# A sorted-token gather cut by blocks: two blocks before the first expert, four between the first four expert steps

## What is computed

```python
scores = sigmoid(h @ w_router)                      # 16 experts in 4 groups of 4
best = argmax over groups of the sum of the two best (scores + b_router) in the group
_, idx = top_k(masked to the best group, 2)
gsel = scores at idx, divided by their sum
combine = one_hot(idx) * gsel                       # a weight for each token and expert
gate, up = split(einsum('ld,edf->lef', xs, w_gu), 2)
hid = silu(gate) * up * combine
out = einsum('lef,efd->ld', hid, w_down)
```

## Time and profile before

| what | value |
|---|---|
| median of the 3 runs | 2985.69 us (2975.92 to 2989.59) |
| the profiled execution | 2981.99 us, of it a span of 2980.2 us |
| mean granted TensorE clock | 0.914 of full speed |
| PE busy | 2643.8 us, 89% |
| DMA | 524.43 MB, 50% of the 16 engines' time on the main queue |

### The profile page before, as it was taken

The page is one execution under the profiler, slowest core; times in us unless marked ns, Lnnn a source line. Parts: engine busy times, 40 slices in busy tenths (PEclk is TensorE's granted clock), DMA queues, the critical chain, the costliest instruction groups (busy, mean ns, idle before and its releaser), DMA issues.

```text
span 2980.2 us, 30519 instructions
## 1 busy us (share of the span) xinstructions
PE 2643.8 (89%) x11934; PEld 1940.3 (65%) x11934; DVE 1462.1 (49%) x2288; ACT 745.8 (25%) x1255; POOL 805.2 (27%) x445
## 2 busy tenths in 40 slices
PE   5688989997997889899998877788999899989997
PEld 3687864445986678744457876676444599974444
DVE  7446443334549876533335578974333416650012
ACT  1132120002453442300014244423010233230111
POOL 3355300002443254000013558850000156500000
PEclk7789889998899999799998887897999999979999
DMA  7534639891330215388953321032989243428881
GB/s 269 170 113 126 201 111 353 323 348 62 105 111 29 71 57 170 113 311 323 350 186 119 128 74 34 20 123 97 350 323 361 100 130 112 141 100 281 297 298 47
DMA packets 291854, 524.43 MB, mean 176 GB/s; under 512 B 9472, under 2 KB 141056, under 8 KB 291328
## 3 DMA queue, kind: packets, MB, share of 16 engines
q1 hardware_dynamic: 288256, 519.33, 50.0%
q10 hardware_dynamic: 3456, 3.15, 0.3%
HBM read 517.73 MB, written 4.72 MB: 175 GB/s over the span
## 4 chain that ended last, share of the span: by engine, by line
PE 75%; DVE 12%; issue 4%; DMA 3%; ACT 3%; POOL 2%; SPq 0%; DVEq 0%; ACTq 0%
PE ps L1755 23%; PE ps L1770 11%; PE ps L1547 6%; PE ps L1549 6%; PE ps L1548 6%; PE ps L1581 3%; DVE macc L1840 3%; PE ps L1617 2%; POOL wlo L1479 2%; PE ps L1570 2%; PE ps L1571 1%; PE ps L1572 1%; DVE h L1870 1%; PE ps L1695 1%; PE ps L1609 1%
## 5 line engine op out<-in xcount | busy, mean ns | idle before, releaser
L1479 POOL TENSOR_TENSOR wlo<-ring,whi 128x1024 fp32r<-128x1024 f32 x202 | 529.0, 2634 | 1546.2 <-ACT whi L1346 1546.1
L1755 PE MATMUL ps<-ring,xg 128*128 128x512 f32 x1536 | 702.5, 602 | 0.0
L1755 PEld LDWEIGHTS ps<-ring,xg 128*128 128x128 f32 x1536 | 288.4, 193 | 326.2 <-issue 325.9
L1840 DVE SCALAR_TENSOR_TENSOR macc<-ring,cond_s,macc 128x1024 f32<-128x1024 f32 x322 | 436.9, 1417 | 10.5 <-DMA ring<-w_mod 10.5
L2051 DVE SCALAR_TENSOR_TENSOR hid<-ps,cws,sg 128x256 f32<-128x256 f32 x96 | 46.5, 484 | 667.9 <-ACT sg L1439 667.9
L1770 PE MATMUL ps<-ring,hidt 128*128 128x512 f32 x768 | 353.9, 604 | 2.3 <-ACT hidt L1413 2.3
L1547 PE MATMUL ps<-hh,whi 128*128 128x384 f32 x832 | 303.2, 364 | 28.2 <-POOL wlo L1479 18.3
L1346 ACT ACTIVATE whi<-ring 128x1024 fp32r<-128x1024 f32 x202 | 206.9, 1053 | 349.8 <-DMA ring<-gmlp_w_out 115.2
L1549 PE MATMUL ps<-hh,wlo 128*128 128x384 f32 x832 | 289.2, 348 | 0.0
L1548 PE MATMUL ps<-hl,whi 128*128 128x384 f32 x832 | 289.2, 348 | 0.0
L1770 PEld LDWEIGHTS ps<-ring,hidt 128*128 128x128 f32 x768 | 148.8, 194 | 190.3 <-issue 190.3
(11 more groups left out here) (327 smaller groups left out, 4185.1 us busy)
## 6 DMA issues: line engine op xcount, KB each, us to landing
ring<-moe_w_gu SPq DMA_DIRECT2D x192, 1024.0 KB, 7.8
ring<-w_mod SPq DMA_DIRECT2D x96, 1024.0 KB, 8.2
ring<-moe_w_down SPq DMA_DIRECT2D x96, 1024.0 KB, 5.7
ring<-gmlp_w_in SPq DMA_DIRECT2D x32, 1024.0 KB, 5.7
ring<-ssd_w_in SPq DMA_DIRECT2D x21, 1024.0 KB, 5.4
ring<-hgrn_w_in SPq DMA_DIRECT2D x20, 1024.0 KB, 5.2
ring<-gmlp_w_out SPq DMA_DIRECT2D x16, 1024.0 KB, 5.9
ring<-ssd_w_out SPq DMA_DIRECT2D x8, 1024.0 KB, 5.9
```

Of the source, the lines that this page charges most:

```text
L1479: pool.tensor_tensor(split_sub(wlo, s0), raw_sub(s0), split_sub(whi, s0).bitcast(F32), ALU.subtract).then_inc(S["lo_ready"], 1)
L1755: ins = pe.matmul(ps[:, s % 2, :], xg[:, w, k, :], whole(what, s, 4)[:, k % 4, :], start=(k == 0), stop=(k == KD - 1))
L1840: ins = dve.scalar_tensor_tensor(out=macc[:, v, :], in0=w[:, k, :], scalar=by, in1=macc[:, v, :], op0=ALU.mult, op1=ALU.add)
```

## The change

The gather is split by blocks. Ahead of the first expert PE gathers only blocks 0 and 1 (FIRST_W = 2; 8 slices, 6 matmuls of 256 columns each, banks 0 to 3 in turn). `gate_up(0)` follows at once. The slot weights and the slot row move behind `gate_up(0)`. Blocks 2 to 5 (8 slices, 6 matmuls of 512 columns each) are gathered two slices at a time at the end of steps 0 to 3, in banks 6 and 3 in turn. PE waits for the first eight copies ahead of step 0 and for all sixteen ahead of step 8; the wait for `cws` at the entry is gone. ACT copies two slices behind the Silu of each of the first four steps.

```diff
+FIRST_W = 2
 # ACT
-                for k in range(KD):
-                    act.wait_ge(S["gather_done"], 16 * l + 2 * k + 1)
-                    act.activation(xg[:, 0:NG, k, :], ps[:, 2 * (k % 2), :]..., ACT.Copy).then_inc(S["xg_ready"], 1)
-                    act.wait_ge(S["gather_done"], 16 * l + 2 * k + 2)
-                    act.activation(xg[:, NG:NW, k, :], ps[:, 2 * (k % 2) + 1, 0:(NW - NG) * P]..., ACT.Copy).then_inc(S["xg_ready"], 1)
+                def gathered(k, a, b, at_bank, n):
+                    act.wait_ge(S["gather_done"], 16 * l + n + 1)
+                    act.activation(xg[:, a:b, k, :], ps[:, at_bank, 0:(b - a) * P]..., ACT.Copy).then_inc(S["xg_ready"], 1)
+                for k in range(KD):
+                    gathered(k, 0, FIRST_W, k % 4, k)
                 for s in range(STEPS):
 ...
                     act.activation(sg[:, s % 2, :], ps[:, s % 2, 0:DE], ACT.Silu).then_inc(S["sg_ready"], 1)
+                    if s < KD // 2:
+                        for k in (2 * s, 2 * s + 1):
+                            gathered(k, FIRST_W, NW, (6, 3)[k % 2], KD + k)
 # PE
+                def gather(k, a, b, at_bank, n):
+                    claim(at_bank, "xg_ready", 16 * l + n + 1)
+                    for t in range(NT):
+                        pe.matmul(ps[:, at_bank, 0:b - a], thi[:, t, k * P:(k + 1) * P], spread[:, t, a:b], ...)
+                        ins = pe.matmul(ps[:, at_bank, 0:b - a], tlo[:, t, k * P:(k + 1) * P], spread[:, t, a:b], ...)
+                    ins.then_inc(S["gather_done"], 1)
                 for k in range(KD):
-                    (two parts for each k: columns 0 to 511 and 512 to 767, banks 2 * (k % 2) and 2 * (k % 2) + 1)
+                    gather(k, 0, FIRST_W * P, k % 4, k)
+                def slot_weights():
+                    (the wait for cw_ready, claim(5, "cws_ready"), the 18 matmuls, the wait for dslot_ready,
+                     claim(6, "srow_ready") and the matmul of the slot row, as they stood here before)
-                pe.wait_ge(S["xg_ready"], 16 * (l + 1))
-                pe.wait_ge(S["cws_ready"], l + 1)
+                pe.wait_ge(S["xg_ready"], 16 * l + KD)
                 for s in range(STEPS):
+                    if s == FIRST_W * EG:
+                        pe.wait_ge(S["xg_ready"], 16 * (l + 1))
                     gate_up(s)
+                    if s == 0:
+                        slot_weights()
                     if s:
                         down(s - 1)
 ...
+                    if s < KD // 2:
+                        for k in (2 * s, 2 * s + 1):
+                            gather(k, FIRST_W * P, NW * P, (6, 3)[k % 2], KD + k)
```

More of the change, by code:

```diff
@@ L1426, in experts @@
                     tokens_high(i)
+                def gathered(k, a, b, at_bank, n):
+                    act.wait_ge(S["gather_done"], 16 * l + n + 1)
+                    act.activation(xg[:, a:b, k, :], ps[:, at_bank, 0:(b - a) * P].rearrange("p (w n) -> p w n", n=P), ACT.Copy).then_inc(S["xg_ready"], 1)
                 for k in range(KD):
-                    act.wait_ge(S["gather_done"], 16 * l + 2 * k + 1)
-                    act.activation(xg[:, 0:NG, k, :], ps[:, 2 * (k % 2), :].rearrange("p (w n) -> p w n", n=P), ACT.Copy).then_inc(S["xg_ready"], 1)
-                    act.wait_ge(S["gather_done"], 16 * l + 2 * k + 2)
-                    act.activation(xg[:, NG:NW, k, :], ps[:, 2 * (k % 2) + 1, 0:(NW - NG) * P].rearrange("p (w n) -> p w n", n=P),
-                                   ACT.Copy).then_inc(S["xg_ready"], 1)
+                    gathered(k, 0, FIRST_W, k % 4, k)
                 for s in range(STEPS):
@@ L1712, in experts @@
                 pe.wait_ge(S["spread_ready"], NT * (l + 1))
-                for k in range(KD):
-                    for part, (a, b) in enumerate(((0, NG * P), (NG * P, NW * P))):
-                        at_bank = 2 * (k % 2) + part
-                        claim(at_bank, "xg_ready", 16 * l + 2 * k + part + 1)
+                def gather(k, a, b, at_bank, n):
+                    claim(at_bank, "xg_ready", 16 * l + n + 1)
+                    for t in range(NT):
+                        pe.matmul(ps[:, at_bank, 0:b - a], thi[:, t, k * P:(k + 1) * P], spread[:, t, a:b], start=(t == 0), stop=False)
+                        ins = pe.matmul(ps[:, at_bank, 0:b - a], tlo[:, t, k * P:(k + 1) * P], spread[:, t, a:b], start=False,
+                                        stop=(t == NT - 1))
+                    ins.then_inc(S["gather_done"], 1)
@@ L1717, in experts @@
+                for k in range(KD):
+                    gather(k, 0, FIRST_W * P, k % 4, k)
+                def slot_weights():
+                    pe.wait_ge(S["cw_ready"], l + 1)
+                    claim(5, "cws_ready", l + 1)
+                    for w in range(NW):
                         for t in range(NT):
-                            pe.matmul(ps[:, at_bank, 0:b - a], thi[:, t, k * P:(k + 1) * P], spread[:, t, a:b], start=(t == 0), stop=False)
-                            ins = pe.matmul(ps[:, at_bank, 0:b - a], tlo[:, t, k * P:(k + 1) * P], spread[:, t, a:b], start=False,
+                            ins = pe.matmul(ps[:, 5, 2 * EG * w:2 * EG * (w + 1)], spread[:, t, w * P:(w + 1) * P], cw8[:, t, :], start=(t == 0),
@@ L1720, in experts @@
                                             stop=(t == NT - 1))
[L1721 to L1732, removed]
+                    ins.then_inc(S["cws_done"], 1)
+                    pe.wait_ge(S["dslot_ready"], l + 1)
+                    claim(6, "srow_ready", l + 1)
+                    pe.matmul(bank(6), ones[:, :], dslot[:, :, :].rearrange("p t n -> p (t n)"), start=True, stop=True).then_inc(S["srow_done"], 1)
```

## The result

The changed kernel takes 2997.8 us (median of 19 runs, 2986.5 to 3006.6), the kernel before 2984.5 us (median of 19). The ratio is 1.0045, with a 95% interval of 1.0034 to 1.0056: slower by 13 us (10 to 17). The range given (2981 to 3004) holds it and the sign is right, but 13 us is more than the 8 that were forecast. The prediction also reckoned that anything under 0.5% would count as no change; with 19 runs of each kernel the slowdown of 0.45% stands clear of zero.

What follows compares the result with a forecast made beforehand. PE was taken as the bound, so moving its work wins 0. Two holes (6.1 us in four layers) plus 2 us for the clock, on a 2985.7 us median, gave 2994 us, 8-in-10 range 2981 to 3004.

Steps and rivals of the forecast that it cites:

- PE is the bound and the change moves its work, so nothing is won.: Gather and experts: first expert starts some 13 us sooner, but the moved work stays on PE; 0 us.
- The sign given in absolute times: Layer 0's profile: first expert product near 409.4, end of its experts 1 to 5 us later than 696.
- The stream rival: Expert weight loads: the stream was the bound and its earlier start pays; 2933 us, or 2972 for a quarter; chance 0.08.
- The hole on the first copies, 0.67 us: Between early gather and first expert: PE waits for ACT's last 256-column copy, 0.67 us a layer.
- The hole on bank 6, 0.85 us: Between slot row and first late gather: PE waits for DVE's copy of the row from bank 6, 0.85 us a layer.
- Nothing for the weight load behind a wait: Second matmul behind each PE wait: lost weight-load overlap put at 0.29 us at most, then counted as nothing.
- The clock at the sums of modulation, +2 us: Behind the one-column modulation sums: the shift changes which sums meet a clock fall; +2 us, ends -5 and +5.
- the two spared sums: Sums of layers 0 and 2 without a clock fall before: now hit, with layer 1 hit once, giving +1.7 us in all.
- The fall behind the slot work: Late gathers at half clock, 1.45 us a layer if short, 3.4 if long; total 3000 to 3008 us; chance 0.18.
- the prediction's own sign: Behind the slot weights: a granted clock of 0.50 anywhere there decides for the clock-fall rival.
- the forecast without a fall: Whole kernel: both holes and the modulation-sum clock term, no clock fall behind the slot work; 2994 us, chance 0.66.

Runs made afterwards that it cites:

- e10: Changed kernel with slot weights and slot row back ahead of the first expert and three of four modulation sums spread; 0.9953 of the kernel before.
- e5: Kernel before with three of the four modulation sums of layers 0 to 2 issued in pieces between the next gate_up's products; 0.9954 of the kernel before.
- e8: Changed kernel with SP's first weight-ring refill in each layer held until two slices of blocks 2 to 5 are copied; 1.0047 of the kernel before.
- e3: Kernel before, gather whole and ahead of the experts, with only slot weights and slot row moved behind the first gate_up; 1.0000 of the kernel before.
- e2: Changed kernel with the late gather's two banks exchanged, bank 3 ahead of bank 6; 1.0006 of the kernel before.
- e4: Kernel before with the slot row's matmul made three times instead of once, 1.46 us more PE work a layer; 1.0015 of the kernel before.
- e9: Changed kernel with bank 3 ahead of bank 6 in the late gather and three of four modulation sums spread; 0.9962 of the kernel before.
- e6: Changed kernel with three of the four modulation sums of layers 0 to 2 spread between the next gate_up's products; 0.9980 of the kernel before.

## Why the prediction was right, and where it was short

*PE is the bound and the change moves its work, so nothing is won.* Right. The first expert starts 8.5 us after the gather's start (404.16 against 395.66) where it was 21.8 us, and 8.6 had been worked out. The sign given in absolute times (a start near 409.4, an end 1 to 5 us later than 696) was not met, 404.16 and 695.6, because this execution reached the gather 5.2 us sooner; counted from the gather, the stage is 4.7 us longer. Steps 1 to 3 are 13.3 us, the 10.5 of before and 2.8 of gather. e10 against e5 shows the cut at no cost and no gain.

*The stream rival.* False. e8 takes 10.4 us of the head start away and nothing changes.

*The hole on the first copies, 0.67 us.* From 403.41 to 404.16 less the 0.12 of a start to start distance is 0.63 us. Right, but in e3 it is too small to be told.

*The hole on bank 6, 0.85 us.* From the row's start to the gather's it is 1.54 us (413.06 to 414.60), where the next product followed 0.73 behind the row before (421.86 to 422.59), so 0.81. Right.

*Nothing for the weight load behind a wait.* Not right, and it can be read from rows. The second matmul behind a wait comes late: in the gather before, 0.57 us behind the first where the next is 0.42 (400.82, 401.39, 401.81). The same stands behind both new holes. The second record of the first expert starts 0.54 us behind the first (404.16, and 404.70 by its load), where two of them are 0.43 apart. Behind the hole on `srow` it is 0.34 against 0.23 in layer 1, where the clock held:

```profile
1268.57 0.50 PE L1721 MATMUL ps<-spread,thi 128*128 128x512 f32 x1 [0.65 <-DVE srow L2050]
1268.91 0.40 PE L1722 MATMUL ps<-spread,tlo 128*128 128x512 f32 x1
1269.14 0.39 PE L1721 MATMUL ps<-spread,thi 128*128 128x512 f32 x1
```

That is 0.1 us behind each hole. It makes 0.73 + 0.92 = 1.65 us a layer, 6.6 in four in place of 6.1, and it agrees with step 0, 13.35 us where the clock held and 12.42 in e2, 0.93 less.

*The clock at the sums of modulation, +2 us.* Steps 5 and 6 of layers 0 and 2 got 3.4 us longer each, those of layer 1 1.7 shorter, a later sum of layer 1 cost 1.7 more, and the last step of layers 0 to 2, with the last sum, gave back 4.5. It comes to +2.2 in the trace. The size was right by luck: each of the two spared sums was charged 1.7 us and cost 3.4, and the 4.5 us that came back at the last sums had no term. That the block of one-column records brings the fall is shown by e5; that the shift chose which sums were hit is not shown (e4).

*The fall behind the slot work, left out of the sum and given 0.18 as a rival.* This is the term that failed. By the prediction's own sign, a granted clock of 0.50 behind the slot weights, this rival happened and the forecast without a fall did not; 2994 lies near the measured 2997.8 because the term is small. The fall came in three of four layers of the profiled execution, 1.3 us each (14.66 against 13.35), near the price given (1.45 for the short form). In layer 1, which had no fall, the clock also rose sooner in the gather, which took 0.5 us less. The sum is then 6.6 + 2.2 + 4.0 - 0.5 = 12.3 us, against 12.0 in the four layers, 11.3 in the spans and 13 in the medians. I had set the row of a sum of modulation, which shows a fall, against the row of the slot work without one, and followed the latter; but that row had dense products behind it, and here there was a hole. e2, e3 and e9, with the slot work among the products and no hole on `srow`, show no fall behind it in 12 layers; the changed kernel, e6 and e8, with the hole, show it in 8 of 12.

What tells the 8 from the 4 can be read from the same traces: when the clock rose in the gather. In the 8 it rose 4.8 to 5.1 us behind the first gather matmul, in the 4 that were spared 3.7 to 4.2. Four layers of e2 and e9 also had the late rise, with the slot work at the same distance from the gather, and no hole on `srow`: none of them fell. This is the comparison of like with like, and it rests the fall on the hole; e3's slot work comes 11 us later. Stretches from 4.3 to 4.7 us behind the first gather matmul: the changed kernel, layer 0 (late rise, then a fall at the hole) and layer 1 (early, spared), and e2, layer 1 (late, no hole, no fall):

```profile
399.96:400.36 0.40, 0.40 (x4) 0.40 (x4) 0.36 (x2) 0.30 (x1) 0.00 (x0) 0.50 0.00 0
1254.44:1254.84 0.40, 0.40 (x6) 0.40 (x5) 0.36 (x2) 0.14 (x1) 0.00 (x0) 1.00 0.00 0
1252.49:1252.89 0.40, 0.40 (x4) 0.40 (x4) 0.36 (x2) 0.30 (x1) 0.00 (x0) 0.50 0.00 0
```

The Trainium skill ("TensorE: Matmul & The Clock Gate", Step-by-step: what each phase is for) says that PE pulls weight loads ahead of running matmuls. The prediction set the loss of that behind a wait at 0.29 us at most and then at nothing. The traces lie between: about 0.1 us behind each of the eight holes, 0.8 us in all where 2.3 was the most.

## What to carry to other kernels

When PE is the bound and nothing on it waits, starting its first useful product sooner wins nothing, and the seams that the old order hid come to light; look for what covered each evacuation before moving it. Choose the PSUM bank of the next work so that it isn't the one still being copied: here that choice was worth 12 us (1.0045 to 1.0006), or 5 with the sums spread, of which the wait itself is 3.7 (0.9 a layer) and the clock most of the rest. A short hole next to narrow matmuls can cost more than the hole, so spread narrow matmuls between dense ones, and give an engine that must idle before dense work some dense work to do.

## What the runs showed of the hardware

- Eighteen matmuls of 8 columns were busy for 2.07 us behind gather matmuls and for 2.47 us behind fp32 products, and cost the same. From the first product to the slot row it is 8.90 us in the changed kernel (404.16 to 413.06), 0.1 of it the late second record. The 6.87 of the products and the 1.93 of the eighteen before make 8.80.
- Behind a wait the second matmul comes late: by 0.10 to 0.11 us at full clock and by 0.15 to 0.16 at half clock, where the load of the first lasts 0.19 and 0.29 us.
- The same hole of 0.8 us brought the clock down in 8 layers of 12 and spared it in 4, with the same instructions around it. All 8 had the late rise of the clock in the gather (4.8 to 5.1 us) and all 4 the early one (3.7 to 4.2). Unless one knows which a layer will have, a price that hangs on the clock is a chance, not a term, and one trace shows one draw.
- Thirty-two one-column records in a block cost up to 3.4 us by a fall of the clock, and no fall came when they stood four at a time between dense products (e5).
